# Two heads' latent keys in one tile, and new orders in the index stage and in stick-breaking

## The reference

```python
h = rms_norm(x, norm_g); proj = h @ w_in      # 1024 -> q, k, v of three branches, gates
# branch a: stick-breaking, 8 heads of 64
z = q k^T / 8; log_1m = where(k < q, log_sigmoid(-z), 0)
a = where(k < q, exp(log_sigmoid(z) + suffix sums of log_1m), 0); y_a = a @ v
# branch b: latent attention (MLA), 8 heads of 64 + 32 rope
q_b = rms_norm(rms_norm(c_q) @ w_uq); kv = rms_norm(c_kv) @ w_ukv
k_b = rms_norm(concat(kv[..., :64], k_pe of all heads)); rope on the last 32 of q_b and k_b
y_b = causal softmax(q_b k_b^T / sqrt(96)) @ kv[..., 64:]
# branch c: index scores = sum_h w_h relu(ix_q . ix_k), top 128 keys of each query,
#           softmax of 8 heads over these with a relative bias, @ v
x = x + (sum over branches of sigmoid(g + gate_b) * ((y * silu(z)) @ w_branch)) @ w_out
```

## Time and profile before

| stage | layer 0, us from the span's start | layer 1 |
|---|---|---|
| start and index stage | 0 to 125 | 680 to 766 |
| stick-breaking | 125 to 258 | 766 to 898 |
| latent attention | 258 to 335 | 898 to 975 |
| branch c, gates, output | 335 to 680 | 975 to 1334 |

### The profile page before, as it was taken

How to read it: one execution, slowest core, us unless ns; L and a number is a source line. 1 busy time by engine, 2 the same in 40 slices (tenths; PEclk the granted TensorE clock), 3 DMA queues, 4 the chain that set the end, 5 groups by cost and what they waited for, 6 DMA issues and landing times.

```text
span 1333.8 us, 17870 instructions
## 1 busy us (share of the span) xinstructions
PE 1268.9 (95%) x6530; PEld 959.7 (72%) x6538; DVE 773.2 (58%) x1572; ACT 609.0 (46%) x1131; POOL 194.4 (15%) x316
## 2 busy tenths in 40 slices
PE   5898999999899999999999999999999999999998
PEld 5556666555578888888888876655556888888887
DVE  5878777888634344434456477878864424434442
ACT  4346566666653232233244365676666322323330
POOL 1372111133420000000000021113343000000000
PEclk9999999999999999999999999999999999999999
DMA  7244012201322333333332312220123322333321
GB/s 219 86 137 100 31 61 48 63 1 40 91 93 95 95 95 108 104 97 103 92 84 78 96 32 64 48 64 1 34 78 112 96 95 64 125 95 95 95 95 63
DMA packets 118568, 109.15 MB, mean 82 GB/s; under 512 B 34512, under 2 KB 101200, under 8 KB 118480
## 3 DMA queue, kind: packets, MB, share of 16 engines
q1 hardware_dynamic: 118480, 107.99, 27.1%
HBM read 100.64 MB, written 7.34 MB: 81 GB/s over the span
## 4 chain that ended last, share of the span: by engine, by line
PE 76%; DVE 9%; ACT 8%; issue 5%; SPq 1%; DMA 1%; POOL 0%; ACTq 0%; DVEq 0%
PE bank L837 20%; PE bank L839 20%; PE bank L838 20%; PE bank L983 3%; PE bank L1151 2%; PE bank L1194 2%; PE bank L1178 2%; PE bank L792 1%; DVE w_lo L729 1%; PE bank L1007 1%; ACT w_hi L723 1%; DVE probs L2043 1%; ACT soft L1482 1%; PE bank L1024 1%; ACT soft L1484 1%
## 5 line engine op out<-in xcount | busy, mean ns | idle before, releaser
L837 PE MATMUL bank<-h_hi,w_hi 128*128 128x512 f32 (+1 forms) x928 | 361.5, 390 | 4.0 <-DVE w_lo L729 2.2
L839 PE MATMUL bank<-h_hi,w_lo 128*128 128x512 f32 (+1 forms) x928 | 353.5, 381 | 0.0
L838 PE MATMUL bank<-h_lo,w_hi 128*128 128x512 f32 (+1 forms) x928 | 353.2, 381 | 0.0
L729 DVE TENSOR_TENSOR w_lo<-raw,w_hi 128x2048 fp32r<-128x2048 f32 (+2 forms) x98 | 189.1, 1931 | 119.4 <-ACT w_hi L723 119.3
L837 PEld LDWEIGHTS bank<-h_hi,w_hi 128*128 128x128 f32 x928 | 176.4, 190 | 50.5 <-issue 12.1
L723 ACT CAST w_hi<-raw 128x2048 fp32r<-128x2048 f32 (+2 forms) x100 | 159.1, 1593 | 112.5 <-PE bank L839 110.1
L839 PEld LDWEIGHTS bank<-h_hi,w_lo 128*128 128x128 f32 x928 | 176.2, 190 | 33.4
L838 PEld LDWEIGHTS bank<-h_lo,w_hi 128*128 128x128 f32 x928 | 176.4, 190 | 32.7 <-issue 1.9
L1666 ACT ACTIVATE gate<-bank,gains 128x512 f32<-128x512 f32 x48 | 33.0, 688 | 166.1 <-PE bank L839 166.1
L2228 POOL TENSOR_SCALAR probs<-probs,stat 128x128 f32<-128x128 f32 (+3 forms) x128 | 76.0, 594 | 147.3 <-DVE stat L1998 139.9
L837 PE MATMUL bank<-br_hi,w_hi 128*128 128x512 f32 x192 | 74.7, 389 | 0.0
(11 more groups left out here) (239 smaller groups left out, 2228.1 us busy)
## 6 DMA issues: line engine op xcount, KB each, us to landing
raw<-in_w_in SPq DMA_DIRECT2D x56, 1024.0 KB, 5.2
raw<-in_w_branch SPq DMA_DIRECT2D x12, 1024.0 KB, 5.2
raw<-in_w_out SPq DMA_DIRECT2D x8, 1024.0 KB, 5.0
bias<-bias_dram SPq DMA_DIRECT2D x16, 256.0 KB, 3.1
bias<-bias_dram SPq DMA_DIRECT2D x16, 192.0 KB, 2.6
x_sb<-in_x SPq DMA_DIRECT2D x4, 512.0 KB, 4.5
...
```

Source lines behind the costliest of these rows:

```text
L729: e.tensor_tensor(w_lo[:, s % RING, a:b], raw[:, s % RAW, a:b], w_hi[:, s % RING, a:b].bitcast(F32), ALU.subtract).then_inc(*lo_signal(nam ...
L837: pe.matmul(out_ap, lh, rh, start=start and i == 0, stop=False)
L838: pe.matmul(out_ap, lh, rl, start=False, stop=False)
L839: mm = pe.matmul(out_ap, ll, rh, start=False, stop=stop and i == n - 1)
```

## The change

Latent keys: `prep_k` takes a pair of heads p, whose 2 x 64 rows fill one tile kp0 to kp3. For that the columns of w_ukv are loaded with all key columns first and then all value columns (two DMAs of 64-column pieces). ScalarE squares the whole tile (`sq_k`, new tile `kp_sq`), POOL adds the squares of k_pe (`squares_k`, tile `k_pe_sq`, two copies of 32 rows and zeros between), and the norm sum uses `per_head` (128 rows) and comes out for both heads at once. `head_k` and `rope_k` still work head by head. An eighth gain column and copies of the rope rows on partitions 0 to 63 serve the odd and even heads. The ring of keys has four tiles. Keys have the bank that held the first query tile, queries the other one, and the first two score banks are swapped, so that unit 1 waits for head 1's key.

Stick-breaking: in steps with i % 4 == 1 the probabilities of step i-1 come before the softplus of step i on ScalarE, and their masks first on POOL; with i % 4 == 2 probabilities and rounding alternate by heads; in step 15 the norm's reciprocal root goes ahead of the softplus; in the last two steps `prep_q(0)` and `pv_of` go forward on TensorE.

Layer 0's start: bias group 3 is made before the index-key copies and group 7 before the split of slab 2. Slab 5 is split before the first index unit (`hi(5)` ahead of `index_relus(0)`, `split_lo` at u == 0 instead of 4). The sine goes between relu groups 3 and 4 and its table change behind group 4; the rope goes into the score sums at units 16 and 20.

The old `first_rope` goes; its five operations are those of the two new functions. Equal lines and the layout of tiles are left out:

```diff
-N_GAINS = 7
+N_GAINS = 8
+K_RING = 4
...
 def dbank(tile):
-    if tile in ("ix_q1", "kh0"):
+    if tile in ("ix_q1", "kp0"):
         return bank[2]
+    if tile.startswith("kp"):
+        return bank[TILE["qh0"] % 2]
+    if tile.startswith("qh") and tile != "qh0":
+        return bank[TILE["qh1"] % 2]
+def bank_before(tile):
+    i = TILE[tile]
+    if tile.startswith("kp"):
+        return (f"kp{int(tile[2]) - 1}" if tile != "kp1" else "qh0",)
+    if tile.startswith("qh") and tile not in ("qh0", "qh1"):
+        return (f"qh{int(tile[2]) - 1}",)
...
 if name == "ukv":
-    return [(slot[:, 0:HEADS * P], w_ukv[l])]
+    src = w_ukv[l].rearrange("p (h n) -> p h n", h=HEADS)
+    v = slot[:, 0:HEADS * P].rearrange("p (c h n) -> p c h n", c=2, h=HEADS)
+    return [(v[:, c, :, :], src[:, :, c * HD:c * HD + HD]) for c in range(2)]
...
+column(e, gains_in, 7, slice(HD, P), mla_k_g[:, 0:NOPE])
...
 def s_bank(u):
-    return bank[2 + u % S_RING] if u < N_MLA else bank[(u - N_MLA) % 4]
+    return bank[3 - u % S_RING] if u < N_MLA else bank[(u - N_MLA) % 4]
...
-if tile == "kh0":
+if tile == "kp0":
-i = TILE[tile]
-back = 2 if i < FIRST_GATE + 2 else 4
-if i >= 2 and i not in (FIRST_GATE + 2, FIRST_GATE + 3):
-    sig, key = reader(dense_tiles[i - back])
+for earlier in bank_before(tile):
+    sig, key = reader(earlier)
...
-def prep_k(h):
-    if h == 0:
+def prep_k(p):
+    if p == 0:
-    b = tile_bank(f"kh{h}")
-    three(b[0:NOPE, :], [(ukv[0][:, h, 0:NOPE], ukv[1][:, h, 0:NOPE], ckv_hi[:, :], ckv_lo[:, :])]
-          ).then_inc(*dense.tick(f"kh{h}"))
+    b = tile_bank(f"kp{p}")
+    two = slice(2 * p * NOPE, (2 * p + 2) * NOPE)
+    three(b[:, :], [(ukv[0][:, two], ukv[1][:, two], ckv_hi[:, :], ckv_lo[:, :])]
+          ).then_inc(*dense.tick(f"kp{p}"))
+    if h >= 2:
+        pe.wait_ge(*act_evac.at(f"qh{h - 1}ln" if h % 2 else f"kp{h // 2}ln"))
-def norm_k(h):
-    pe.wait_ge(*act_evac.at(f"kh{h}sq"))
-    pe.wait_ge(*act_evac.at(f"qh{h}ln"))
-    norm(f"kh{h}", ones, k_sq, k=QK)
+def norm_k(p):
+    pe.wait_ge(*pool_work.at(f"kp{p}sq"))
+    pe.wait_ge(*act_evac.at(f"qh{2 * p - 1 if p else 0}ln"))
+    norm(f"kp{p}", per_head, kp_sq)
...
+if i == STEPS:
+    prep_q(0)
+if i >= 2:
+    pv_of(i - 2)
-if i >= 2:
-    pv_of(i - 2)
-if i == STEPS:
-    prep_q(0)
...
 if br == "mla":
+    if u == 1:
+        pe.wait_ge(*dve_evac.at("kh1"))
-    pe.matmul(b[:, 0:w], q_head[:, h % 2, q], k_head[:, h % 2, 0:w], start=True, stop=True)
+    pe.matmul(b[:, 0:w], q_head[:, h % 2, q], k_head[:, h % K_RING, 0:w], start=True, stop=True)
...
-if h + 1 < HEADS:
-    if t == 0:
-        prep_k(h + 1)
-    if t == 2 and h + 2 < HEADS:
-        prep_q(h + 2)
+if h % 2 == 0 and t == 0 and h + 2 < HEADS:
+    prep_k(h // 2 + 1)
+if t == 2 and h + 2 < HEADS:
+    prep_q(h + 2)
-if h + 1 < HEADS:
-    if i == 0:
-        norm_q(1)
-    if t == 1:
-        norm_k(h + 1)
-    if t == 3 and h + 2 < HEADS:
-        norm_q(h + 2)
+if i == 0:
+    norm_q(1)
+if h % 2 == 0 and t == 2 and h + 2 < HEADS:
+    norm_k(h // 2 + 1)
+if t == 3 and h + 2 < HEADS:
+    norm_q(h + 2)
...
-e.activation(k_sq[64:96, :], dbank("k_pe")[64:96, :], ACT.Square).then_inc(*act_evac.tick("k_pe"))
+e.activation(k_pe_sq[0:32, :], dbank("k_pe")[64:96, :], ACT.Square).then_inc(*act_evac.tick("k_pe low"))
+e.activation(k_pe_sq[64:96, :], dbank("k_pe")[64:96, :], ACT.Square).then_inc(*act_evac.tick("k_pe"))
...
+hi(5)
-hi(5)
+e.wait_ge(*angle_step.at("angle"))
+e.activation(ang[64:P, :], turns[64:P, :], ACT.Sin).then_inc(*cos_done.tick("sin"))
+e.preload_act_table_set("natural_log_exp_and_others")
...
-if layer.l == 0:
-    e.wait_ge(*angle_step.at("angle"))
-    e.activation(ang[64:P, :], turns[64:P, :], ACT.Sin).then_inc(*cos_done.tick("sin"))
-    e.preload_act_table_set("natural_log_exp_and_others")
...
-def sq_k(h):
-    e.wait_ge(*dense.at(f"kh{h}"))
-    if h:
-        e.wait_ge(*norm_sum.at(f"kh{h - 1}"))
-    e.activation(k_sq[0:NOPE, :], dbank(f"kh{h}")[0:NOPE, :], ACT.Square).then_inc(*act_evac.tick(f"kh{h}sq"))
+def sq_k(p):
+    e.wait_ge(*dense.at(f"kp{p}"))
+    if p:
+        e.wait_ge(*norm_sum.at(f"kp{p - 1}"))
+    e.activation(kp_sq[:, :], dbank(f"kp{p}")[:, :], ACT.Square).then_inc(*act_evac.tick(f"kp{p}sq"))
-def rs_k(h):
-    if h == 0:
+def rs_k(p):
+    if p == 0:
     else:
-        e.wait_ge(*dve_evac.at(f"kh{h - 1}"))
-        e.wait_ge(*pool_work.at(f"kh{h - 1}rope"))
-    rs_of(f"kh{h}", QK, k_rs[:, :])
+        e.wait_ge(*dve_evac.at(f"kh{2 * p - 1}"))
+        e.wait_ge(*pool_work.at(f"kh{2 * p - 1}rope"))
+    rs_of(f"kp{p}", QK, k_rs[:, :])
...
-def rounded(p):
+def rounded(p, head=None):
     for u, o, pair, kt, w in stick_units(p):
+        if head not in (None, o):
+            continue
-def stick_probs(p):
+def stick_probs(p, head=None):
     for u, o, pair, kt, w in stick_units(p):
+        if head not in (None, o):
+            continue
...
+if i % ST == 1:
+    stick_probs(i - 1)
+if i == STEPS - 1:
+    norm_scale(NORM_AT[i])
-early = i % 2 == 0 and i % ST
+early = i % ST == 2
 if early:
-    rounded(i)
+    for head in range(2):
+        stick_probs(i - 1, head)
+        rounded(i, head)
-if NORM_AT.get(i) in EARLY:
+if NORM_AT.get(i) in EARLY and i < STEPS - 1:
-if i:
+if i and i % ST in (0, 3):
...
-if h + 1 < HEADS:
-    if i == 0:
-        rs_q(1)
-        sq_k(1)
-    if t == 1:
-        rs_k(h + 1)
-    if t == 2 and h + 2 < HEADS:
+if i == 0:
+    rs_q(1)
+if h + 2 < HEADS:
+    if h % 2 == 0 and t == 0:
+        sq_k(h // 2 + 1)
+    if t == 2:
-    if t == 3 and h + 2 < HEADS:
+    if h % 2 == 0 and t == 2:
+        rs_k(h // 2 + 1)
+    if t == 3:
...
+def first_rope_products():
+    rows, low_rows = slice(64, 96), slice(96, P)
+    e.wait_ge(*cos_done.at("sin"))
+    e.wait_ge(*gains_in.at("b", DEPTH - 1, 2))
+    e.tensor_scalar(cos_sin[64:P, :], ang[64:P, :], sign[64:P, :], None, ALU.mult).then_inc(*setup_dve.tick("cs"))
+    e.wait_ge(*setup_dve.at("cs"))
+    e.scalar_tensor_tensor(turns[rows, :], k_rope[low_rows, :], gain[low_rows, 4:5], cos_sin[low_rows, :],
+                           ALU.mult, ALU.mult).then_inc(*dve_evac.tick("kr2"))
+    e.scalar_tensor_tensor(k_rope[rows, :], k_rope[rows, :], gain[rows, 4:5], cos_sin[rows, :],
+                           ALU.mult, ALU.mult).then_inc(*dve_evac.tick("kr0"))
+def first_rope_sums():
+    rows, low_rows = slice(64, 96), slice(96, P)
+    e.wait_ge(*dve_evac.at("kr0"))
+    e.tensor_tensor(k_rope[low_rows, :], k_rope[rows, :], turns[rows, :], ALU.add).then_inc(*dve_evac.tick("kr1"))
+    e.tensor_tensor(k_rope[rows, :], k_rope[rows, :], turns[rows, :], ALU.add).then_inc(*dve_evac.tick("kr"))
+    e.wait_ge(*dve_evac.at("kr"))
+    e.tensor_copy(k_rope[0:64, :], k_rope[64:P, :]).then_inc(*dve_evac.tick("kr low"))
+if layer.l == 0:
+    reaches(e, 3, 4)
...
-reaches(e, 3, 7)
+reaches(e, 4, 7)
+reaches(e, 7, 8)
-reaches(e, 7, 11)
+reaches(e, 8, 11)
...
 for u, (h, t) in enumerate(INDEX_UNITS):
-    if layer.l == 0 and u == 4:
+    if layer.l == 0 and u == 0:
+    if layer.l == 0 and u == 16:
+        first_rope_products()
+    if layer.l == 0 and u == 20:
+        first_rope_sums()
...
+e.wait_ge(*dve_evac.at("kr"))
+e.tensor_copy(k_rope[0:64, :], k_rope[64:P, :]).then_inc(*dve_evac.tick("kr low"))
...
 def head_k(h):
-    e.wait_ge(*act_evac.at(f"kh{h}rs"))
-    if h >= 2:
-        e.wait_ge(*logits.at(4 * (h - 2) + 3))
-    e.scalar_tensor_tensor(k_head[0:NOPE, h % 2, :], dbank(f"kh{h}")[0:NOPE, :], gain[0:NOPE, 4:5],
-                           k_rs[0:NOPE, :], ALU.mult, ALU.mult).then_inc(*dve_evac.tick(f"kh{h}"))
+    e.wait_ge(*act_evac.at(f"kp{h // 2}rs"))
+    if h >= K_RING:
+        e.wait_ge(*logits.at(4 * (h - K_RING) + 3))
+    r, g = (slice(0, NOPE), 4) if h % 2 == 0 else (slice(HD, P), 7)
+    e.scalar_tensor_tensor(k_head[0:NOPE, h % K_RING, :], dbank(f"kp{h // 2}")[r, :], gain[r, g:g + 1],
+                           k_rs[r, :], ALU.mult, ALU.mult).then_inc(*dve_evac.tick(f"kh{h}"))
...
+head_k(1)
...
-if h + 1 < HEADS:
-    if t == (0 if h else 1):
-        head_q(h + 1)
-    if t == 2:
-        head_k(h + 1)
+if h + 1 < HEADS and t == (0 if h else 1):
+    head_q(h + 1)
+if h % 2 == 0 and h + 2 < HEADS and t == 3:
+    head_k(h + 2)
+if h % 2 and h + 2 < HEADS and t == 1:
+    head_k(h + 2)
...
+def mask_probs(p):
+    for u, o, pair, kt, w in stick_units(p):
+        d = stick_a[:, o, 0:P]
+        e.wait_ge(*stick_prob.at(u))
+        e.affine_select(out=d, in_=d, pattern=[[1, P]], compare_op=ALU.is_gt, fill=0.0, base=0,
+                        channel_multiplier=-1).then_inc(*prob_masked.tick(u))
 for i in range(STEPS + 1):
+    if i % ST == 1:
+        mask_probs(i - 1)
-    if i:
-        for u, o, pair, kt, w in stick_units(i - 1):
-            d = stick_a[:, o, 0:P]
-            e.wait_ge(*stick_prob.at(u))
-            e.affine_select(out=d, in_=d, pattern=[[1, P]], compare_op=ALU.is_gt, fill=0.0, base=0,
```

(46 more changed lines are left out.)

25 lines of the change are left out of this document (8 added, 17 removed).

## The result

The changed kernel takes 1319.4 us (median of 4 runs, 1318.9 to 1320.1) where the one before takes 1337.8 on the same chip: ratio 0.9864, 95% interval 0.9847 to 0.9881. Its profiled execution took 1319.59 us, span 1317.7. That is 18.4 us by the medians and 15.9 between the two profiled executions; 28 were forecast.

The account below looks back on a forecast made before the run. TensorE, busy 95%, was taken as the bound. Terms 4.0 + 2.0 + 6.0 + 16.0 = 28 us off the profiled 1335.52 gave 1307.5, or 1309.5 for the median; range for 8 in 10: 1301 to 1322.

Parts of the forecast that it names:

- the likeliest course: Whole kernel: the summed gains come about as forecast, by itself 1302 to 1317 us; chance 0.61.
- rival 2: Latent attention: POOL's squares block VectorE through the shared port, eight operations of 1.27 us, 10.2 us, so 1320; chance 0.09.
- Start: First 50 us: earlier bias tiles shorten two TensorE gaps (1.7, 1.8) and avoid a clock fall (1.7); 4.0 us net.
- half split: Start: the 2.5 us split now stands before bias groups 8 to 10; half of it charged as loss, 1.2 us.
- Index stage: Layer 0: shorter relu wait (1.0), 2.40 us gap cut to leave 0.5, clock gain 0.5; sum 2.0 us, bounds 0 and 4.5.
- Stick-breaking: Both layers: earlier probabilities and masks remove TensorE waits, 3.9 us per layer, taken as 3.0 because removed waits often return.
- Rival 4: Stick-breaking: ScalarE is held at 8 places where i%4==2, costing 37.6 us, so slower at 1347; chance 0.04.
- Latent attention: Both layers: pairing keys removes projections, norm sums and square waits; 8.0 us per layer, 16 in all, bounds 5.5 and 10.5.
- Queue work: Latent loop, TensorE: four key projections (2.8 us) and four norm sums (3.4 us) fewer per layer.
- The waits for the key squares: Latent stage: 5.3 us per layer of TensorE waits, gone but for 0.5; queueing behind VectorE takes back perhaps 2.
- Entry: Start of the latent stage: TensorE stands about 0.9 instead of 0.5 us for squares going over POOL; -0.4 us.
- rival 1: VectorE takes over: latent stage gives 4 us per layer, stick-breaking nothing; 12 us in all, 1325.7; chance 0.16.

Follow-up runs that it names:

- the first four experiments: The kernel before with one part alone: latent-key pairing, stick-breaking order, layer 0's index-stage order, or bias-tile order; 1336.2, 1331.9, 1334.9 and 1330.8 us.

## Why the prediction was right, and where it was wrong

**Direction and range** held, but 1319.4 lies outside what the likeliest course alone allowed (1302 to 1317); the range holds it because it was widened for rival 2. That the time is so near rival 2's 1320 is chance: that rival priced POOL's additions at 10.2 us, and taking them out gave 3.6. The sum was 9.6 us too high against the medians, 12 against the profiled executions. The 2.5 us between the two are probably the clock: the profiled execution of before had two falls in the first 135 us, two others with its gaps had four, and of the two traces of the changed kernel one has none there and one has one. Times and clock go together: in the 30 executions of before beside the first four experiments with a mean granted clock of 0.991 to 0.997, those at 0.991 took 1339.8 us on average, those at 0.995 1336.8 and those at 0.997 1333.4.

**Start**, 4.9 for 4.0: right, by the same terms. The first gap gave its 1.7 (36.31 to 34.59). The second gap and the clock together gave 4.0, not 3.5: from 36.31 to 45.80 it was 9.5 us, from 34.59 to 40.04 it is 5.5. Of the half split charged against it (1.2), 0.8 came due. It shows as no wait of its own, but the bias matmuls of the groups behind the split now go at the pace at which VectorE makes their tiles, one in 0.26 us (the row of before, then of after):

```profile
50.39 0.61 PE L792 MATMUL bank<-reach_u,step_w 128*32 128x256 f32 x8
```

```profile
44.73 1.32 PE L816 MATMUL bank<-reach_u,step_w 128*32 128x256 f32 x8
```

From the first of these groups to the matmul behind the last it takes 2.24 us (43.74 to 45.98) where it took 1.43 (49.50 to 50.93).

**Index stage**, 1.8 and 0.8 behind it, against 2.0. The relu wait gave the forecast 1.0 (1.98 to 0.96). The 2.40 us gap gave 1.05 and the split of slab 6 took 0.77 back, about what its term said. That TensorE waits for this split was one of the forecast's signs of being wrong, and it showed at 119.59. The 0.8 behind the stage is the clock, 1.5, less this wait. The clock's part was partly luck: it was forecast at 0.5, and in six of the nine traces with this gap the clock falls. The mark "below 1.2 us" at that place was missed (1.35), as was "below 0.6" at 36 (1.05). ScalarE's table loads took 1.28 us each, as the sum assumed. The Trainium skill, page "ScalarE: Activation LUTs", section "What ACT_TABLE_LOAD costs", gives the load itself some 1.28 us and puts the rest of the 2.7 that the prediction quotes in a drain beside it; the trace agrees on the load (1.28 us at 120.62) and shows no drain behind it, as the sine starts at 121.92.

**Stick-breaking**, 2.1 and 2.5 for 3.0. TensorE's own waits for probabilities and masks, before and after, layer 0:

```profile
PE bank L997 <- ACT stick_a L1500: 3.3, 4, 1.3
PE bank L1024 <- POOL stick_a L2204: 2.5, 3, 1.6
```

```profile
PE bank L1019 <- ACT stick_a L1529: 1.7, 2, 0.9
PE bank L859 <- DVE ds_q L1929: 1.4, 1, 1.4
...
PE bank L1046 <- POOL stick_a L2248: 0.2, 1, 0.2
```

5.8 us became 1.9, and 1.4 came new, at the last step's query projection, which now stands ahead of the product and waits for VectorE's `ds_q`. The deduction for a wait that comes back was right in size. That this term came out is partly luck: its 11.3 us were waits of the weight loads, about twice TensorE's own 5.8, and the mark "under 6 us" was met by TensorE's own rows before the change. Rival 4 is out, since the stage became shorter.

**Latent attention**, 2.6 for 8.0 per layer, is the step that failed. Its terms, which add up to 8.6 and not to the 8.0 that was written (2.8 + 3.4 + 5.3 - 0.5 - 2 - 0.4):
1. Queue work: 2.8 + 3.4 = 6.2 forecast, 5.6 measured. Near.
2. "The waits for the key squares are 5.3 us per layer": that row is of the weight loads. At one and the same wait their row can show more than the matmul's, since the matmul before is still running (at entry of the changed kernel 1.75 and 0.87 us). TensorE's own row says 3.9, and the stage's whole idle time was 4.1. And they did not go: idle time rose to 6.5. The forecast let the waits fall by 2.8 (5.3, less 0.5 and 2 for VectorE); they rose by 2.4. These 5.2 us are nearly all of the miss.
3. Entry: -0.4 forecast, -0.6 measured. TensorE stands 0.9 us for POOL's addition, as forecast, and without the addition the entry is as short as without the pairing (21.3 us both). In the old order of the last steps that wait is 1.9 us and the entry loses 1.7.

In place of term 2 the runs showed a chain over three engines. VectorE's queue feeds it (2.35 us per layer go with top-k), POOL's addition lengthens VectorE's product where they meet, and ScalarE's order puts the squares behind it.

So rival 1 was half true, without VectorE being the bound: it is 86% busy (56.76 of 66.29), but what counts is where its maxima stand. Rival 2 was true at two places per layer, not four: the cosine product took 1.65 us for 0.69 with the additions of the first two pairs of keys; both operations have two operands in SBUF. With the third and fourth pair's, POOL's addition started 0.1 to 0.2 us behind VectorE's product and itself took 1.7 us. The additions' whole price, with POOL's own time, was 3.6 us, not 10.2. The Trainium skill, page "SBUF — State Buffer", section "SBUF: two separate sides", has this as an exclusive lock, and the trace agrees: in these rows whoever comes second takes longer. The row maximum behind the product reads a bank and begins 0.04 us after the product ends (261.50), which looks like the queue's order alone; no run parts it.

**Loads and the new copy.** No wait for the new loads shows. "In layer 1 the new copy lies in VectorE's slack" was wrong by 0.4 us: the wait for the relu there grew from 0.51 to 0.97, and the index stage of layer 1 is 0.4 to 0.5 longer in every kernel with the pairing and in none of the three without. One more wait, 0.68 us for `norm_out` at 702.16, is new there too; ScalarE's second square of the rope keys, not costed in the prediction, is the likely cause, but no run parts it.
